# One plain gate-up chunk fewer per feed-forward block, and another place for the sums of input quarters

## The reference

```python
D_FF = -(-8 * D_MODEL // (3 * 256)) * 256        # 2816
# block 0, at the end of the first layer
hn = rms_norm(h, norm2_g)
gate, up = jnp.split(hn @ w_gate_up, 2, axis=-1)
return h + (jax.nn.silu(gate) * up) @ w_down
# blocks 1 and 2, the second layer
def swiglu(h, w_gate, w_up, w_down):
    return (jax.nn.silu(h @ w_gate) * (h @ w_up)) @ w_down
x = x + 0.5 * swiglu(rms_norm_2(x, ffn1_norm[i]), ...)
x = x + 0.5 * swiglu(rms_norm_2(x, ffn2_norm[i]), ...)
```

## Time and profile before

| | |
|---|---|
| median of three runs | 1967.1 us (1965.23 to 1967.56) |
| profiled execution: its time | 1966.0 us |
| profiled execution: its span | 1964.2 us |
| TensorE matmul | 1946.3 us busy, 99% of the span, 11449 matmuls |
| TensorE weight load | 1719.8 us, 88% |
| VectorE | 1197.6 us, 61% |
| GpSimd | 1134.5 us, 58% |
| ScalarE | 931.3 us, 47% |
| bytes moved by DMA | 189.68 MB, mean 97 GB/s |

### The profile page before, as it was taken

How to read it: one execution, slowest core, us unless ns; L and a number is a source line. 1 busy time by engine, 2 the same in 40 slices (tenths; PEclk the granted TensorE clock), 3 DMA queues, 4 the chain that set the end, 5 groups by cost and what they waited for, 6 DMA issues and landing times.

```text
span 1964.2 us, 30689 instructions
## 1 busy us (share of the span) xinstructions
PE 1946.3 (99%) x11449; PEld 1719.8 (88%) x11449; DVE 1197.6 (61%) x2067; ACT 931.3 (47%) x1649; POOL 1134.5 (58%) x915
## 2 busy tenths in 40 slices
PE   9999999999999999999999999999999999999999
PEld 8998887888899989879998988889888888999977
DVE  6588665635647455775755656677645565646574
ACT  6413225533536435454552644667644463634532
POOL 5344442254667657557775756666554566766663
PEclk9999999999999999999999999999999999999999
DMA  5222331123333333323333332332222333333331
GB/s 179 91 87 91 102 94 56 44 86 107 87 108 103 113 86 108 102 71 108 108 108 88 107 108 87 107 101 79 77 89 86 94 94 106 106 113 91 108 109 75
DMA packets 253850, 189.68 MB, mean 97 GB/s; under 512 B 6608, under 2 KB 249680, under 8 KB 253680
## 3 DMA queue, kind: packets, MB, share of 16 engines
q1 hardware_dynamic: 253024, 187.53, 32.0%
q10 hardware_dynamic: 688, 0.31, 0.1%
HBM read 180.93 MB, written 2.10 MB: 93 GB/s over the span
## 4 chain that ended last, share of the span: by engine, by line
PE 88%; DVE 5%; ACT 3%; issue 3%; POOL 1%; DMA 0%; DVEq 0%; SPq 0%; ACTq 0%
PE ps L793 18%; PE ps L794 18%; PE ps L795 18%; PE ps L944 9%; PE ps L945 9%; PE ps L946 9%; PE ps L1133 1%; PE ps L1285 1%; DVE tmp L1891 1%; ACT whi L1350 1%; PE ps L1205 1%; PE ps L1206 1%; PE ps L1207 1%; DVE hT L2076 1%; PE ps L1273 1%
## 5 line engine op out<-in xcount | busy, mean ns | idle before, releaser
L631 POOL TENSOR_TENSOR wlo<-raw,whi 128x512 fp32r<-128x512 f32 (+2 forms) x420 | 547.2, 1335 | 532.2 <-ACT whi L1350 411.3
L793 PE MATMUL ps<-xh,whi 128*128 128x512 f32 (+1 forms) x1008 | 380.3, 377 | 1.7 <-POOL wlo L631 1.7
L795 PE MATMUL ps<-xh,wlo 128*128 128x512 f32 (+1 forms) x1008 | 372.9, 370 | 0.0
L794 PE MATMUL ps<-xl,whi 128*128 128x512 f32 (+1 forms) x1008 | 372.7, 370 | 0.0
L1350 ACT ACTIVATE whi<-raw 128x2048 fp32r<-128x2048 f32 (+1 forms) x86 | 160.8, 1869 | 335.5 <-PE ps L795 287.1
L654 POOL TENSOR_TENSOR wlo<-raw,whi 128x512 fp32r<-128x512 f32 x162 | 213.2, 1318 | 152.6 <-ACT whi L1404 152.4
L793 PEld LDWEIGHTS ps<-xh,whi 128*128 128x128 f32 x1008 | 189.5, 188 | 33.4 <-POOL wlo L631 2.5
L795 PEld LDWEIGHTS ps<-xh,wlo 128*128 128x128 f32 x1008 | 189.3, 188 | 33.0
L794 PEld LDWEIGHTS ps<-xl,whi 128*128 128x128 f32 x1008 | 189.9, 188 | 28.4 <-issue 0.7
L793 PE MATMUL ps<-fh,whi 128*128 128x512 f32 x528 | 205.9, 390 | 1.6 <-POOL fl L643 1.6
L794 PE MATMUL ps<-fl,whi 128*128 128x512 f32 x528 | 205.6, 389 | 0.0
(11 more groups left out here) (385 smaller groups left out, 4900.1 us busy)
## 6 DMA issues: line engine op xcount, KB each, us to landing
raw<-in_w_in SPq DMA_DIRECT2D x87, 512.0 KB, 4.5
raw<-in_w_gate_up SPq DMA_DIRECT2D x44, 512.0 KB, 5.0
raw<-in_ffn_w_gate SPq DMA_DIRECT2D x44, 512.0 KB, 4.0
raw<-in_ffn_w_up SPq DMA_DIRECT2D x44, 512.0 KB, 5.3
raw<-in_ffn_w_down SPq DMA_DIRECT2D x32, 512.0 KB, 4.3
raw<-in_w_down SPq DMA_DIRECT2D x16, 512.0 KB, 4.1
raw<-in_ffn_w_down SPq DMA_DIRECT2D x16, 384.0 KB, 3.4
raw<-in_w_b SPq DMA_DIRECT2D x8, 512.0 KB, 3.9
```

Of the source, the lines that this page charges most:

```text
L631: ins = pool.tensor_tensor(wlo[:, c % 2, cs], raw[:, c % 2, cs], whi[:, c % 2, cs].bitcast(F32), ALU.subtract)
L793: pe.matmul(o, w_of(whi), xhi, start=first, stop=False)
L794: pe.matmul(o, w_of(whi), xlo, start=False, stop=False)
L795: return pe.matmul(o, w_of(wlo), xhi, start=False, stop=last)
```

## The change

`PLAIN` goes from 4 to 3: tile 3 of every block, chunk p = 3, is folded where it was plain. There are 19 folded chunks in a block in place of 18. As folding begins a chunk earlier, the forms are moved: in blocks 0 and 2 from (0), (1, 2), (3) in turns 0, 1, 2 to (0, 1), (2, 3) in turns 0 and 1; in block 1 from (0, 1), (2, 3) in turns 1 and 2 to (0), (1, 2, 3) in turns 0 and 1.

```diff
 DOWN_K = (6, 8, 8)
 UPS = (7, 8, 7)
-PLAIN = 4
+PLAIN = 3
 RING = 9
...
-FORMS_AT = ({0: (0,), 1: (1, 2), 2: (3,)}, {1: (0, 1), 2: (2, 3)})
+FORMS_AT = ({0: (0, 1), 1: (2, 3)}, {0: (0,), 1: (1, 2, 3)})
```

## The result

The changed kernel takes 1979.3 us (median of 4 runs, 1978.7 to 1979.7), the kernel before 1967.0 in the same comparison (median of 4): the ratio is 1.0065, 95% interval 1.0053 to 1.0077. It is slower by 12.3 us, or 0.6%.

What follows compares the result with a forecast made beforehand. TensorE was taken to bound the kernel, holding 88% of the chain that ended last. Block terms 2.55 + 2.24 + 4.89 = 9.7 us on 1966.0 gave 1975.7; with 1.1 for the median, 1976.8 us, range 1973 to 1981.

Steps and rivals of the forecast that it cites:

- my own signs of being wrong: L1350 of p2 as early as before, block 1's p3 without a hole, or a granted-clock stretch at 1.2 GHz.
- The spacing, 0.91 us a chunk: On TensorE, a folded chunk takes 9.97 us against 10.88 plain: 0.91 us less in each block, 2.7 in all.
- the form ahead of L1350: A second form delays p2's high halves by 3.46 us; net +2.55 us in block 0, +2.24 in block 2.
- The copies were in time in both: Blocks 0 and 2, p3: ScalarE's product copies in time, the third by 0.4 and 0.5 us; nothing added.
- Block 1: Late p2 and waits for copies inside p3: +4.89 us, the saved 0.91 and lost wait before p3 included.
- the steps up to p2: Block 1: L1938 takes 0.69 us, L1350 comes at 854.72, not 849.43; p2 waits 3.92 us, restart included.
- The term for the copies: Block 1, inside p3: TensorE waits 2.46 us for the first product's copy and 0.5 for the third, 0.1 restart each.
- the rival to which I gave 0.15: Clock falls in the new holes, ten matmuls costing 2 us: one or two falls 1978.8 to 1980.8, three 1982.8; chance 0.15.
- block 1 was not milder: Rival: in block 1 ScalarE's chain catches up or later waits absorb part of the delay: about 1973.6 us; chance 0.09.
- none of the forecast waits stayed away: Rival: the second form hides and no wait appears, not slower; 1963.1 us with no added wait; chance 0.04.
- A new wait beside those named: Rival: an unseen wait, such as the reload of the raw slots, put 3.5 us later: above 1981 us; chance 0.04.

Runs made afterwards that it cites:

- Experiment 1: Kernel before, four plain chunks kept, with only the forms moved to the changed kernel's turns: 1981.6 us.
- Experiment 3: Changed kernel with 15, 14 and 10 overwritten matmuls filling TensorE's idle time ahead of p2 in blocks 0, 1 and 2: 1976.0 us.
- experiment 2: Changed kernel with forms as late as possible: one ahead of p2's high halves in blocks 0 and 2, all four behind in block 1: 1977.3 us.
- experiment 4: Changed kernel with ScalarE's high halves of p2 put ahead of the forms of turn 0: 1980.1 us.
- Experiment 5: Against the kernel before: blocks 0 and 2 have three plain chunks and form 0 ahead of the root, block 1 as before: 1964.2 us.
- experiment 6: Experiment 5 with three plain chunks and the changed kernel's forms in block 1 too: 1970.0 us.

## Why the prediction was right

The direction, the holes' places and their sizes came as forecast, and 1979.3 us lies inside the range of 1973 to 1981. It lies outside the band of 1975 to 1978.5 that had the chance of 0.68, and one of my own signs of being wrong came true: the granted clock shows stretches at 1.2 GHz. In the profiled execution the parts are 9.68 us as summed, 2.28 and 1.38 for the clock, which the sum had at nothing, -0.20 from the blocks' other terms, and -0.64 from stretches without a change: 12.5 us of span.

**The spacing, 0.91 us a chunk:** right. Experiment 1 against the change gives 1.00 and 0.94 us.

**Blocks 0 and 2, the form ahead of L1350:** right in place and size. The second form came 3.47 us behind the first, and L1350 3.46 us later against p0. Block 2 lost 2.17 us where 2.24 was worked out. Block 0 lost 4.84; with the 12 matmuls at half clock in 5.00 us taken at 0.2267 each (2.28 us less) it is 2.56 where 2.55 was worked out. The copies were in time in both, as forecast.

**Block 1:** the sum was right, 4.75 against 4.89, and the steps up to p2 to some hundredths (L1938 0.69, L1350 at 21.82 us behind p0). The term for the copies was mis-sized in this trace: 2.46 and 0.5 us were worked out, 0.64 and 0.35 measured. The low clock behind p2's hole made TensorE come 1.6 us later to p3, so that ScalarE's lateness was shared between the two. Experiment 3, with that low clock away, measured 2.19 for the first copy. The third product of p3 started 45.12 us behind p0's first matmul in the changed kernel and 45.11 in experiment 3 (835.19 to 880.30); 45.18 had been worked out. So the half-clock stretch ahead of a chain that TensorE waits for anyhow cost nothing of its own there.

**The clock:** the rival to which I gave 0.15 is what happened, beside the forecast and not in its place. It fell behind p2's holes of blocks 0 and 1 but not behind block 2's, and added 2.3 us in block 0, nothing in block 1, and 1.4 in the second group of block 1. The warning of the Trainium skill that was cited (TensorE: Matmul & The Clock Gate, Why this matters for your kernels) agrees with the traces for the holes of 4.1 and 3.6 us. The wait ahead of the fall at 961.5 was 2.4 us, shorter than the gaps of which that section warns, and there the measurement decides. The rival's 1980.8 lay nearer to the 1979.3 measured than my 1976.8, but in part by luck: of its two falls only block 0's cost time, and the 1.4 us came where nobody had looked. The three falls that it priced at 1982.8 did occur. The step that fell short is the sum's clock, taken as full because no longer hole was in the rows; the holes that I had worked out myself were reason to put more weight on it.

**The other rivals:** block 1 was not milder, and none of the forecast waits stayed away. A new wait beside those named did not come in the changed kernel; in experiments 2 and 4 it did (VectorE's release of the accumulator).

## What to carry to other kernels

Work that is moved ahead of an operand's preparation is paid by the engine that waits for the operand, and what it costs is the length of its dialogue between engines (3.46 us for a form), not its busy time; its place is where both engines of the dialogue already wait. A hole in TensorE can have a second price, the clock behind it: here 2.3 us behind 4.1 us of idling, and nothing behind 2.8 us. So a worked-out hole of some microseconds should be costed with one stretch at half clock as a rival sum. That price counts only where TensorE does not have to wait for another engine a moment later anyhow.

## What was not expected of the hardware

The same wait of 2.4 us in block 1's second group left the clock full in the profiled executions of the kernel before and of experiments 1, 3 and 4, and was followed by 1.2 GHz in those of the changed kernel and of experiments 2, 5 and 6. What decides between the two is open. Repeated runs of one kernel differ in the same way, though their clocks are on record only as means, which don't say where they fell: of 21 runs of the kernel before in one comparison, 5 at a mean granted clock of 1.000 took 1965.2 to 1965.6 us, and 16 at 0.999 took 1966.2 to 1967.4. The kernel before's profiled execution had no fall and lay 1.1 us under the median, but at 1966.0 us it is also 0.4 us above the slowest of those five; that rest is not explained. Of experiment 5's runs, 6 at 1.000 took 1963.4 to 1964.2, and 5 at 0.999 took 1964.8 to 1965.9: at equal clock 1.6 to 1.7 us faster than the kernel before (medians 1963.7 and 1965.4, 1965.2 and 1966.8), where 1.8 was worked out.
